# Attention: twelve copies of stacked queries and keys made by VectorE in place of ScalarE

## The chip, the cores and the metric

One core of a Trainium2 chip. The metric is the device time of one execution in microseconds. Of the kernel before there are three runs, and one execution more that the hardware profiler recorded.

## The reference, cut to what matters

A decoder layer: a mixer of four parallel groups (differential attention, a Conformer convolution, a short gated convolution, causal pooling) behind one input projection, an output projection, then an MLP with a squared ReLU. The change lies in the attention. It has 4 heads with two maps each; queries and keys have 32 elements a map, values 64 a head.

```python
sc = jnp.einsum('bhmqd,bhmkd->bhmqk', qi, k).astype(jnp.float32) * scale
mask = kpos[None, :] <= (st + jnp.arange(Q_BLOCK))[:, None]
p = jax.nn.softmax(jnp.where(mask, sc, -jnp.inf), axis=-1)
a = p[:, :, 0] - lam * p[:, :, 1]
return jnp.einsum('bhqk,bhkd->bhqd', a.astype(v.dtype), v)
```

The sequence has 2048 rows, so 16 row tiles of 128. Row tile i attends to i + 1 tiles of keys.

## The kernel before, in words

The kernel runs in phases: the input projection with the convolutions, attention, the output projection, the MLP. In attention a unit u is one head of one row tile (i = u // 4, head u % 4), and there are 64 of them. A loop over steps 0 to 66 is written out for each engine; each engine works its own list in order, and semaphores tie the lists together. In step u:

- **TensorE** (`score`, `turn`, `product`, and the loop below them) takes the score matmuls of unit u, one item for each map at first (L2421, with a mask product on the diagonal, L2424), and between them the items of `at_items(u)`: the transposes of `turn` (L2386). One kind of them, "stack", prepares the next row tile: in step u the quarter f = u % 4 of row tile u // 4 + 1, f = 0 and 1 its queries (four of the eight maps each), f = 2 and 3 its keys. The other kind, "at", transposes the attention weights of unit u - 3. Their PSUM banks, 4 and 5, alternate, so item n waits until item n - 2 has been read. `product` (L2401) multiplies the turned weights with the values, two items later.
- **VectorE** (`read_scores`, L1837) reads each score item out of PSUM, scales it and takes the row minimum; between the two reads it does `combine(u - 2)` (L1854, L1855, L1857), which makes a = p0 - ratio * p1. Behind the reads of steps 0 to 3 it runs taps of the convolution (`pump`, L1615, four in a step for u < 3, and the last one with two sums, L1626, in step 3), later parts of a layer norm (L1640, L1641, L1654, L1659).
- **ScalarE** takes the exponentials of unit u - 1 (`exp_of`, L1267) and between them the first half of the step's items (`read_turn`, L1258): each item is copied out of PSUM, a stack item into `q_stack` or `k_stack`, a weights item into `a_t`. The second half follows the second exponential. In some steps it also makes the rounded heads of the queries and keys (`split_head`, L1235), whose remainders POOL computes (L941), and in steps 7 and 8 the layer norm's square and root, with table loads.

Three waits hold this together. A score item waits until the item two before it has been read (`sc_read`). Before the first unit of a row tile TensorE waits until the tile's last stack item has been read. A turn waits for the read of the turn two before. All reads of turns raise one semaphore, `at_read`, whose count is the number of the item in `AT_ITEMS`.

The layer norm adds two items: column sums of 128x512 (L2298) at step 6 in place of a score, and at step 8 in place of a turn.

```python
for k in range(max(pairs, len(items))):
    if k < pairs:
        score(u, k)
    if k < len(items):
        turn(items[k])
        behind.append(items[k])
        if len(behind) > 2:
            product(behind.pop(0))
```

Of the kernel before, what the change touches and what calls it, by code (L numbers as in the profile page):

```python
# [23 lines left out]
P = 128  # L24
# [6 lines left out]
BLK = 512  # L31
# [68 lines left out]
UNITS = NT * HEADS  # L100
# [47 lines left out]
def running(counts):  # L148
    out = [0]
    for n in counts:  # L150
        out.append(out[-1] + n)
    return out
# [8 lines left out]
SC_NO = running(len(sc_items(u)) for u in range(UNITS))  # L161
AT_ITEMS = [x for u in range(-1, STEPS) for x in at_items(u)]
AT_POS = {x: n for n, x in enumerate(AT_ITEMS)}
PV_NO = running(len(at_groups(u)) for u in range(UNITS))
UPPER_NO = running(int(upper(u) < len(at_groups(u))) for u in range(UNITS))
SLOT = [3, 1, 2, 0]


def turned(u):
# [11 lines left out]
def trunk(nc, x, c, w_ada, b_ada, norm1_g, norm2_g, w_in, w_out, q_norm_g, k_norm_g, lam_params,  # L181
# [3 lines left out]
    with ctx:  # L185
# [7 lines left out]
        def sem(name):  # L193
# [149 lines left out]
        split_hi, split_lo = sem("split_hi"), sem("split_lo")  # L343
        sc_mm, sc_read, max_ready, exp_done, a_ready = [sem(n) for n in (
            "sc_mm", "sc_read", "max_ready", "exp_done", "a_ready")]
        at_mm, at_read, pv_mm, o_read = [sem(n) for n in ("at_mm", "at_read", "pv_mm", "o_read")]
        upper_ready = sem("upper_ready")
        asq_ready, ams_ready, arms_ready, arcp_ready, att_ready = [sem(n) for n in (
            "asq_ready", "ams_ready", "arms_ready", "arcp_ready", "att_ready")]
# [29 lines left out]

        def chan_no(h, cc, b):  # L380
            return (h * NB + b) * GC + cc

        def prob(u, m, c0, n):

# [46 lines left out]
        def ln_read(h, b, s):  # L431

            if (h, b) == (1, 1):
                return (at_read, AT_POS["ln", 1, 1] + 1) if s else (sc_read, SC_NO[LN_STEP] + 1)
            return (lnsd_ready if s else lnd_ready), h * NB + b + 1

        def released(o):
# [134 lines left out]
        def _(sp):  # L572
# [169 lines left out]

            def store_att(j):
                if j < LAST:
                    sp.wait_ge(at_read, AT_POS["att", j, 1] + 1)
                else:
                    sp.wait_ge(last_read, 2)
                src = att_t[j % 2] if j < LAST else att_t_last
                sp.dma_start(mix_v[:, 0:2, j * BLK:(j + 1) * BLK], src[:, :, :]).then_inc(attt_st[j % 2], 16)
# [242 lines left out]
        def _(act):  # L992
# [244 lines left out]
            def read_turn(x):  # L1237
                kind, i, f = x
                n = AT_POS[x]
                if kind == "ln":  # L1240
                    ln_root(1, 1)
                    return
                act.wait_ge(at_mm, n + 1)
                width = BLK
                if kind == "stack":
                    m0, width = 4 * (f % 2), BLK
                    src = at_bank(n).rearrange("p (m t) -> p m t", m=4)
                    dst = q_stack[i % 2][:, m0:m0 + 4, :] if f < 2 else k_stack[:, m0:m0 + 4, i * P:(i + 1) * P]
                elif kind == "att":
                    if i >= 2 and f == 0:  # L1250
                        act.wait_ge(attt_st[i % 2], 16)
                    src, dst = at_bank(n), att_t[i % 2][:, f, :]
                else:
                    gn, width = PV_NO[i] + f, at_groups(i)[f][1] * P
                    if gn >= 3:
                        act.wait_ge(pv_mm, gn - 2)
                    src, dst = at_bank(n)[:, 0:width], a_t[gn % 3][:, 0:width]
                A(dst, src, ACT.Copy).then_inc(at_read, 1)  # L1258
# [36 lines left out]
            for u in range(STEPS):  # L1295
                for n, a in splits_at(u):
                    split_head(n, a)
                if u == LN_STEP + 1:
                    ln_square(1, 1)
                if u in (LN_STEP + 10, LN_STEP + 11):  # L1300
                    ln_silu(1, 1, (u - LN_STEP - 10,))
                items = at_items(u)
                early = (len(items) + 1) // 2
                if 0 <= u - 1 < UNITS:
                    exp_of(u - 1, 0)
                for n, x in enumerate(items[:early]):
                    read_turn(x)
                    if u == UNITS + 1:
                        if n == 0:
                            act.wait_ge(sc_mm, SC_NO[UNITS])  # L1310
                        mix_head(n)
                if 0 <= u - 1 < UNITS:
                    exp_of(u - 1, 1)
                for n, x in enumerate(items[early:]):
                    if n == 0 and u == UNITS + 1:
                        wo_head(0, 0, (at_mm, turned(UNITS - 3)))
                    read_turn(x)
                if u == UNITS + 2:
                    wo_head(0, 1, (at_mm, turned(UNITS - 2)))
# [142 lines left out]
        def _(dve):  # L1462
# [397 lines left out]
            def read_o(i):  # L1860
                if i >= 8 and i % 4 == 0:
# [5 lines left out]
                                in1=inv_sum[:, i % 4, :].rearrange("p (a o) -> p a o", o=1).to_broadcast([P, HEADS, VD])  # L1867
                                ).then_inc(o_read, 1)

            def mix_tail(n):  # L1870
                tok = slice(n % HT * P, (n % HT + 1) * P)
                dve.wait_ge(mixhi_ready, n + 1)
                V.tensor_tensor(out=h_lo[:, :, tok], in0=mix_in[n % 2][:, :, :], in1=f32(h_hi[:, :, tok]),
                                op=ALU.subtract).then_inc(mix_ready, 1)
# [21 lines left out]
            for u in range(STEPS):  # L1896
                if u == FULL:
                    for b in range(NB):
                        dve.wait_ge(ln_st[b], 32)
                older = (lambda: combine(u - 2)) if 0 <= u - 2 < UNITS else (lambda: None)  # L1900
                if u < UNITS:
                    read_scores(u, older)
                else:
                    older()
                if u >= 8 and u % HEADS == 0 and u // HEADS - 2 < NT:
                    read_o(u // HEADS - 2)

                pump(taps, 4 if u < 3 else 9 * TAPS)
                if 0 <= u - LN_STEP - 3 < 4:
                    inverted = ln_inverse(u - LN_STEP - 3)  # L1910
                if 0 <= u - LN_STEP - 7 < GC:
                    ln_scale_part(u - LN_STEP - 7, inverted)
                j = att_stage(u, 1)
                if j is not None:
                    att_sums(j, att_sq)
                    first_guess(j)
# [286 lines left out]
        def _(pe):  # L2203
# [158 lines left out]
            def turn(x):  # L2362
                kind, i, f = x
                n = AT_POS[x]
                if n >= 2:
                    pe.wait_ge(at_read, n - 1)
                if kind == "ln":
                    ln_sum(1, 1, 1).then_inc(at_mm, 1)
                    return
                if kind == "stack":  # L2370
                    a = f // 2
                    pe.wait_ge(split_lo, 2 * i + a + 1)
                    src = f32((k_split if a else q_split)[:, :, :, :]).rearrange("p m s d -> p m (s d)")
                    srcs = [src[:, 4 * (f % 2) + m, :] for m in range(4)]
                elif kind == "att":
                    pe.wait_ge(att_ready, i + 1)
                    srcs = [att_tiles(i)[:, t, f * P:(f + 1) * P] for t in range(4)]
                else:
                    k0, nk = at_groups(i)[f]
                    if f == 0:  # L2380
                        pe.wait_ge(a_ready, i + 1)
                    if f == upper(i):
                        pe.wait_ge(upper_ready, UPPER_NO[i] + 1)
                    srcs = [prob(i, 0, (k0 + k) * P, P) for k in range(nk)]
                for m, src in enumerate(srcs):
                    ins = nc.tensor.transpose(at_bank(n)[:, m * P:(m + 1) * P], src, ident[:, :])  # L2386
                ins.then_inc(at_mm, 1)

            def product(x):
                kind, u, g = x  # L2390
                if kind != "at":
                    return
                i, hd = u // HEADS, u % HEADS
                gn, (k0, nk) = PV_NO[u] + g, at_groups(u)[g]
                pe.wait_ge(at_read, AT_POS[x] + 1)
                if u == 0:
                    pe.wait_ge(v_ld, 16)
                if hd == 0 and g == 0 and i >= 2:
                    pe.wait_ge(o_read, i - 1)
                for k in range(nk):  # L2400
                    ins = M(psum[:, 6 + i % 2, hd * VD:(hd + 1) * VD], a_t[gn % 3][:, k * P:(k + 1) * P],  # L2401
                            v_sb[:, k0 + k, hd * VD:(hd + 1) * VD], start=(k0 + k == 0), stop=(k0 + k == i),
                            skip_group_check=True)
                ins.then_inc(pv_mm, 1)
# [28 lines left out]
            for u in range(STEPS):  # L2433
                pairs, items = len(sc_items(u)), at_items(u)
                if u < UNITS and u % HEADS == 0:
                    pe.wait_ge(at_read, AT_POS["stack", u // HEADS, 3] + 1)
                for k in range(max(pairs, len(items))):
                    if k < pairs:
                        score(u, k)
# [19 lines left out]
                            skip_group_check=(t == 0))  # L2459
                return ins  # L2460

            pe.wait_ge(at_read, len(AT_ITEMS))
            for hc in range(2):
                n0 = hc * HT
                for t in range(HT):
# [148 lines left out]
```

## Time and profile before

| | us |
|---|---|
| median of three runs | 2356.99 |
| lowest, highest | 2356.3, 2362.84 |
| profiled execution | 2356.43 |
| its span | 2354.6 |
| attention, first score to last transposes | about 493 to 838 |
| granted TensorE clock, mean over the span | 0.993 |

Engines in the profile: PE is TensorE, PEld its weight loads, DVE VectorE, ACT ScalarE, POOL GpSimd, SPq the queue of DMAs that SyncE issues. A granted clock of 1.00 is 2.4 GHz, 0.50 is 1.2 GHz. In a timeline row the bracket gives the engine's idle time before the instruction and what ended it. A read with a minimum (TENSOR_SCALAR_CACHE_REDUCE) is followed by a short DVE_READ_ACCUMULATOR.

### The profile page before, as it was taken

How to read it: one execution, taken by the hardware profiler on the slowest of the kernel's cores; microseconds unless marked ns; L12 is line 12 of the kernel's file. 1: busy time of each engine (PE TensorE's matmuls, PEld its weight loads, DVE VectorE, ACT ScalarE, POOL GpSimd, SP SyncE). 2: the span in 40 equal slices, each digit the busy share in tenths (PEclk: the TensorE clock that was granted, in tenths of full speed). 3: DMA queues.
4: the chain of work that ended last, by engine and by line, in shares of the span. 5: the costliest groups of instructions: out<-in, count | busy, mean ns of one | idle time of the engine just before them, and what ended most of it. 6: DMA issues, size and time to landing. Idle time of an engine off the chain costs nothing.

```text
span 2354.6 us, 31383 instructions
## 1 busy us (share of the span) xinstructions
PE 2283.8 (97%) x11642; PEld 1924.3 (82%) x11642; DVE 1746.0 (74%) x2659; ACT 971.2 (41%) x1595; POOL 357.9 (15%) x285
## 2 busy tenths in 40 slices
PE   6999999988999999999999999999999999999999
PEld 5987898767889888888888888888888888888887
DVE  6648886889989876876767767676787676767676
ACT  4531555458888844332323232233432323222231
POOL 0442044824356610000000000000000000000000
PEclk9999999989999999999999999999999999999999
DMA  7441533120000152011111111145111111111112
GB/s 270 155 152 63 157 129 118 63 89 28 15 10 24 52 155 81 18 54 54 53 53 53 37 61 45 54 132 189 63 36 53 54 36 62 45 53 53 53 53 89
DMA packets 108280, 177.68 MB, mean 75 GB/s; under 512 B 5512, under 2 KB 77468, under 8 KB 107164
## 3 DMA queue, kind: packets, MB, share of 16 engines
q1 hardware_dynamic: 108100, 176.41, 22.6%
q8 instruction: 58, 0.95, 0.2%
q14 instruction: 34, 0.28, 0.0%
q10 hardware_dynamic: 88, 0.04, 0.0%
HBM read 152.84 MB, written 23.59 MB: 75 GB/s over the span
## 4 chain that ended last, share of the span: by engine, by line
PE 81%; DVE 10%; DMA 3%; issue 2%; ACT 2%; POOL 2%; SPq 0%; ACTq 0%; DVEq 0%; POOLq 0%
PE ps L2513 10%; PE ps L2512 10%; PE ps L2511 10%; PE ps L2550 8%; PE ps L2548 8%; PE ps L2549 8%; PE ps L2210 5%; PE ps L2212 5%; PE ps L2211 5%; PE ps L2401 3%; DVE ps L1615 2%; PE ps L2458 2%; PE ps L2456 2%; PE ps L2457 2%; DMA sb_w_raw<-in_w_in 2%
## 5 line engine op out<-in xcount | busy, mean ns | idle before, releaser
L1997 DVE TENSOR_TENSOR sb_x_new<-sb_x_new,ps 128x512 f32<-128x512 f32 x512 | 347.2, 684 | 107.5 <-PE ps L2513 102.0
L2511 PE MATMUL ps<-sb_w_hi,sb_u_hi 128*128 128x512 f32 x1024 | 398.3, 389 | 0.0
L2512 PE MATMUL ps<-sb_w_lo,sb_u_hi 128*128 128x512 f32 x1024 | 398.3, 389 | 0.0
L2513 PE MATMUL ps<-sb_w_hi,sb_u_lo 128*128 128x512 f32 x1024 | 398.3, 389 | 0.0
L2512 PEld LDWEIGHTS ps<-sb_w_lo,sb_u_hi 128*128 128x128 f32 x1024 | 192.2, 188 | 39.9
L2511 PEld LDWEIGHTS ps<-sb_w_hi,sb_u_hi 128*128 128x128 f32 x1024 | 192.2, 188 | 39.9
L2513 PEld LDWEIGHTS ps<-sb_w_hi,sb_u_lo 128*128 128x128 f32 x1024 | 192.2, 188 | 39.9
L2212 PE MATMUL ps<-sb_h_hi,sb_w_lo 128*128 128x512 f32 x512 | 199.4, 389 | 0.0
L1428 ACT ACTIVATE ps<-ps 128x512 f32<-128x512 f32 x28 | 16.3, 582 | 410.8 <-PE ps L2550 410.8
L2210 PE MATMUL ps<-sb_h_hi,sb_w_hi 128*128 128x512 f32 x448 | 177.5, 396 | 0.7 <-DVE sb_w_lo L1958 0.7
L2211 PE MATMUL ps<-sb_h_lo,sb_w_hi 128*128 128x512 f32 x448 | 174.4, 389 | 0.0
L2548 PE MATMUL ps<-sb_h_hi,sb_ring_hi 128*128 128x512 f32 x448 | 174.3, 389 | 0.0
L2549 PE MATMUL ps<-sb_h_lo,sb_ring_hi 128*128 128x512 f32 x448 | 174.3, 389 | 0.0
L1354 ACT ACTIVATE sb_u_hi<-sb_u_full 128x512 fp32r<-128x512 f32 x128 | 81.0, 632 | 192.0 <-DVE sb_u_full L1986 114.2
L1837 DVE TENSOR_SCALAR_CACHE_REDUCE sb_scores<-ps 128x1024 f32<-128x1024 f32 (+7 forms) x160 | 139.5, 891 | 12.4 <-PE ps L2424 6.9
L2401 PE MATMUL ps<-sb_v_sb,sb_a_t 128*128 128x64 f32 x1088 | 140.7, 270 | 0.0
L1615 DVE SCALAR_TENSOR_TENSOR ps<-sb_conf,sb_col,ps 128x512 f32<-128x512 f32 x208 | 140.4, 747 | 0.0
L2401 PEld LDWEIGHTS ps<-sb_v_sb,sb_a_t 128*128 128x128 f32 x1088 | 136.4, 195 | 0.5 <-ACT sb_q_stack L1258 0.2
L2421 PE MATMUL ps<-sb_k_stack,sb_q_stack 128*128 128x512 f32 (+3 forms) x320 | 112.8, 417 | 23.2 <-DVE sb_scores L1837 18.3
L2550 PE MATMUL ps<-sb_h_hi,sb_w_lo 128*128 128x512 f32 x336 | 130.7, 389 | 0.0
L2548 PE MATMUL ps<-sb_w_hi,sb_ring_hi 128*128 128x512 f32 x336 | 130.7, 389 | 0.0
L2549 PE MATMUL ps<-sb_w_lo,sb_ring_hi 128*128 128x512 f32 x336 | 130.7, 389 | 0.0
(291 smaller groups left out, 4947.9 us busy)
## 6 DMA issues: line engine op xcount, KB each, us to landing
sb_w_full<-in_w_ff SPq DMA_DIRECT2D x34, 1024.0 KB, 4.9
sb_w_full<-in_w_ff SPq DMA_DIRECT2D x56, 512.0 KB, 3.7
sb_w_raw<-in_w_in SPq DMA_DIRECT2D x16, 1024.0 KB, 5.6
sb_ada<-in_w_ada SPq DMA_DIRECT2D x32, 512.0 KB, 5.0
sb_ada_first<-in_w_ada SPq DMA_DIRECT2D x8, 1024.0 KB, 13.7
sb_x_in<-in_x SPq DMA_DIRECT2D x16, 512.0 KB, 5.4
sb_mix_in<-mix_scratch SPq DMA_DIRECT2D x16, 512.0 KB, 4.9
sb_x_new<-in_x SPq DMA_DIRECT2D x16, 512.0 KB, 4.9
```

Source lines behind the costliest of these rows:

```text
L1615: ins = V.scalar_tensor_tensor(out=dst, in0=src, scalar=w, in1=dst, op0=ALU.mult, op1=ALU.add)
L1997: V.tensor_tensor(out=y, in0=y, in1=psum[:, 4 + p % 4, :], op=ALU.add).then_inc(ff2_read, 1)
L2210: M(dst, ah, bh, start=(n == 0), stop=False)
L2211: M(dst, ah, bl, start=False, stop=False)
L2212: ins = M(dst, al, bh, start=False, stop=(n == last))
L2401: ins = M(psum[:, 6 + i % 2, hd * VD:(hd + 1) * VD], a_t[gn % 3][:, k * P:(k + 1) * P], v_sb[:, k0 + k, hd * VD:(hd + 1) * VD], start=(k0 ...
L2511: M(dst, uh, wh[:, j, col], start=j == order[0], stop=False, skip_group_check=fast)
L2512: M(dst, uh, wl[:, j, col], start=False, stop=False, skip_group_check=fast)
L2513: ins = M(dst, ul, wh[:, j, col], start=False, stop=j == order[1], skip_group_check=fast)
L2548: M(psum[:, bank, :], wh[:, k, :], rh[:, k, :], start=fresh and k == 0, stop=False, skip_group_check=True)
L2549: M(psum[:, bank, :], wh[:, k, :], rl[:, k, :], start=False, stop=False, skip_group_check=True)
L2550: ins = M(psum[:, bank, :], wl[:, k, :], rh[:, k, :], start=False, stop=k == DC // 2 - 1, skip_group_check=True)
```

## The change

A list `BY_DVE` marks twelve stack items: all four quarters of row tiles 1 and 2 and the key quarters (f = 2, 3) of row tiles 3 and 4. They fall in steps 0 to 7, 10, 11, 14 and 15. VectorE copies them (`copy_stack`) behind `combine(u - 2)`, between its score reads, and raises `stack_read`. ScalarE's list leaves them out, and is halved after leaving them out. Every wait for the read of a turn goes through `turn_read(n)`, which names the semaphore that counts item n and its number there. TensorE waits at the start of a row tile for both its last query quarter and its last key quarter.

```diff
+BY_DVE = [x[0] == "stack" and (1 <= x[1] <= 2 or 3 <= x[1] <= 4 and x[2] > 1) for x in AT_ITEMS]
+AT_BY_DVE = running(int(d) for d in BY_DVE)
...
+def stacks_of_dve(u):
+
+    return [x for x in at_items(u) if BY_DVE[AT_POS[x]]]
...
+        def stacked(i, f):
+
+            m0 = 4 * (f % 2)
+            return (at_bank(AT_POS["stack", i, f]).rearrange("p (m t) -> p m t", m=4),
+                    q_stack[i % 2][:, m0:m0 + 4, :] if f < 2 else k_stack[:, m0:m0 + 4, i * P:(i + 1) * P])
+
+        def turn_read(n):
+
+            by_dve = AT_BY_DVE[n + 1]
+            return (stack_read, by_dve) if BY_DVE[n] else (at_read, n + 1 - by_dve)
...
-                items = at_items(u)
+                items = [x for x in at_items(u) if not BY_DVE[AT_POS[x]]]
                 early = (len(items) + 1) // 2
...
+            def copy_stack(i, f):
+                src, dst = stacked(i, f)
+                dve.wait_ge(at_mm, AT_POS["stack", i, f] + 1)
+                V.tensor_copy(dst, src).then_inc(stack_read, 1)
...
-                older = (lambda: combine(u - 2)) if 0 <= u - 2 < UNITS else (lambda: None)
+                def older():
+                    if 0 <= u - 2 < UNITS:
+                        combine(u - 2)
+                    for x in stacks_of_dve(u):
+                        copy_stack(*x[1:])
+
                 if u < UNITS:
                     read_scores(u, older)
...
                 if n >= 2:
-                    pe.wait_ge(at_read, n - 1)
+                    pe.wait_ge(*turn_read(n - 2))
...
                 if u < UNITS and u % HEADS == 0:
-                    pe.wait_ge(at_read, AT_POS["stack", u // HEADS, 3] + 1)
+                    pe.wait_ge(*turn_read(AT_POS["stack", u // HEADS, 1]))
+                    pe.wait_ge(*turn_read(AT_POS["stack", u // HEADS, 3]))
```

The other waits for `at_read` (the layer norm's, `store_att`, `product`, and the one before the output projection) are rewritten with `turn_read` in the same way.

VectorE's list from the first score read on, steps 0 to 2, before (L1837 reads a score, L1615 is a convolution tap):

```order
L1837 TENSOR_SCALAR sb_scores_128,sb_part_min<-ps 128x128 [waits sc_mm,proj_ready]
L1837 TENSOR_SCALAR sb_scores_128,sb_part_min<-ps 128x128 [waits sc_mm]
L1615 SCALAR_TENSOR_TENSOR ps<-sb_conf,sb_col_55,ps 128x512 [waits dve_chain] x4
L1837 TENSOR_SCALAR sb_scores_128,sb_part_min<-ps 128x128 [waits sc_mm] x2
L1615 SCALAR_TENSOR_TENSOR ps<-sb_conf,sb_col_55,ps 128x512 [waits dve_chain] x4
L1837 TENSOR_SCALAR sb_scores_129,sb_part_min<-ps 128x128 [waits sc_mm]
L1854 RECIPROCAL sb_ratio<-sb_exp_sum 128x1 [waits exp_done]
L1855 SCALAR_TENSOR_TENSOR sb_ratio<-sb_exp_sum,sb_ratio,sb_small 128x1 [waits dve_chain]
L1857 SCALAR_TENSOR_TENSOR sb_scores_128<-sb_scores_128,sb_ratio 128x128 [waits dve_chain]
```

and now, from the first copy on (L1853 reads a score, L1889 is the copy):

```order
L1889 CAST sb_q_stack_136<-ps 128x512 [waits at_mm]
L1853 TENSOR_SCALAR sb_scores_128,sb_part_min<-ps 128x128 [waits sc_mm]
L1631 SCALAR_TENSOR_TENSOR ps<-sb_conf,sb_col_55,ps 128x512 [waits dve_chain] x4
L1853 TENSOR_SCALAR sb_scores_128,sb_part_min<-ps 128x128 [waits sc_mm]
L1889 CAST sb_q_stack_136<-ps 128x512 [waits at_mm]
L1853 TENSOR_SCALAR sb_scores_128,sb_part_min<-ps 128x128 [waits sc_mm]
L1631 SCALAR_TENSOR_TENSOR ps<-sb_conf,sb_col_55,ps 128x512 [waits dve_chain] x4
L1853 TENSOR_SCALAR sb_scores_129,sb_part_min<-ps 128x128 [waits sc_mm]
L1870 RECIPROCAL sb_ratio<-sb_exp_sum 128x1 [waits exp_done]
L1871 SCALAR_TENSOR_TENSOR sb_ratio<-sb_exp_sum,sb_ratio,sb_small 128x1 [waits dve_chain]
L1873 SCALAR_TENSOR_TENSOR sb_scores_128<-sb_scores_128,sb_ratio 128x128 [waits dve_chain]
L1889 CAST sb_k_stack<-ps 128x4x128 [waits at_mm]
```

A copy stands between the two reads of each step, behind the combination where there is one.

TensorE's list from the last key quarter of row tile 1 (step 3) to the second score of step 4, before (L2386 transposes, L2421 is a score, L2424 its mask product):

```order
L2386 MATMUL ps<-sb_ident,sb_k_split 128x128 [waits split_lo,at_read]
L2386 MATMUL ps<-sb_ident,sb_k_split 128x128 x3
L2421 MATMUL ps<-sb_k_stack,sb_q_stack_135 128x128 [waits sc_read]
L2424 MATMUL ps<-sb_mask_r,sb_ident_r 128x128
L2386 MATMUL ps<-sb_ident,sb_scores_128 128x128 [waits a_ready,at_read]
L2421 MATMUL ps<-sb_k_stack,sb_q_stack_136 128x256 [waits sc_read,at_read]
L2424 MATMUL ps<-sb_mask_r,sb_ident_r 128x128
L2386 MATMUL ps<-sb_ident,sb_q_split 128x128 [waits split_lo,at_read]
L2386 MATMUL ps<-sb_ident,sb_q_split 128x128 x3
L2421 MATMUL ps<-sb_k_stack,sb_q_stack_136 128x256 [waits sc_read]
L2424 MATMUL ps<-sb_mask_r,sb_ident_r 128x128
```

and now:

```order
L2412 MATMUL ps<-sb_ident,sb_k_split 128x128 [waits split_lo,stack_read]
L2412 MATMUL ps<-sb_ident,sb_k_split 128x128 x3
L2447 MATMUL ps<-sb_k_stack,sb_q_stack_135 128x128 [waits sc_read]
L2450 MATMUL ps<-sb_mask_r,sb_ident_r 128x128
L2412 MATMUL ps<-sb_ident,sb_scores_128 128x128 [waits a_ready,stack_read]
L2447 MATMUL ps<-sb_k_stack,sb_q_stack_136 128x256 [waits sc_read,stack_read]
L2450 MATMUL ps<-sb_mask_r,sb_ident_r 128x128
L2412 MATMUL ps<-sb_ident,sb_q_split 128x128 [waits split_lo,stack_read]
L2412 MATMUL ps<-sb_ident,sb_q_split 128x128 x3
L2447 MATMUL ps<-sb_k_stack,sb_q_stack_136 128x256 [waits sc_read]
L2450 MATMUL ps<-sb_mask_r,sb_ident_r 128x128
```

Nothing has moved; the first score of row tile 1 (128x256) and the transposes around it now wait for `stack_read`, which VectorE raises.

## Rows read from the trace of the kernel before

**Rows 1.** the page, busy time: us, share of the span, instructions
```profile
PE 2283.8 (97%) x11642; PEld 1924.3 (82%) x11642; DVE 1746.0 (74%) x2659; ACT 971.2 (41%) x1595; POOL 357.9 (15%) x285
```

**Rows 2.** stretches: length, busy PE, PEld, DVE, ACT, POOL, clock, DMA share, GB/s
```profile
485.00:506.20 21.20, 14.38 (x73) 11.86 (x71) 20.92 (x46) 11.99 (x29) 9.30 (x8) 0.74 0.60 196
506.20:512.90 6.70, 6.68 (x23) 4.81 (x24) 2.76 (x14) 4.27 (x15) 1.27 (x1) 0.54 0.17 48
...
523.20:541.30 18.10, 13.36 (x92) 10.89 (x92) 17.64 (x48) 14.76 (x40) 3.82 (x3) 1.00 0.06 16
```

**Rows 3.** chain of waits, 486 to 560 us: start us, us, what
```profile
495.25 2.64 DVE ps L1615 x4
...
498.30 2.64 DVE ps L1615 x4
...
506.22 0.58 PE ps L2421
...
512.91 0.69 DVE sb_acc L1640
...
515.77 0.60 ACT sb_scores L1267 x2
...
523.18 0.17 DVE sb_ratio L1854
...
541.34 0.03 ACT sb_scores L1267
```

**Rows 4.** TensorE alone, microsecond stretches: busy time, granted clock, DMA share
```profile
492.00:493.00 1.00, 0.00 (x0) 1.00 0.00 0
...
495.00:496.00 1.00, 0.91 (x5) 0.63 0.83 313
...
512.00:513.00 1.00, 1.00 (x7) 0.84 0.00 0
```

**Rows 5.** ScalarE's copy line; then timeline of VectorE: start us, us, instruction
```profile
L1258 ACT ACTIVATE sb_k_stack<-ps x32: 573/580/610, 490.7 to 781.6; 128x512 fp32r<-128x512 f32 x32
...
483.49 0.48 DVE L1697 TENSOR_SCALAR sb_stage<-sb_prod,sb_col 128x512 f32<-128x512 f32 x1
...
509.12 0.42 DVE L1837 TENSOR_SCALAR_CACHE_REDUCE sb_scores<-ps 128x256 f32<-128x256 f32 x1
...
536.99 0.68 DVE L1837 TENSOR_SCALAR_CACHE_REDUCE sb_scores<-ps 128x512 f32<-128x512 f32 x1
537.60 0.08 DVE L1837 DVE_READ_ACCUMULATOR sb_scores<-ps 128x1 f32 x1
```

**Rows 6.** timeline of TensorE and VectorE, steps 3 to 5
```profile
504.28 0.55 PE L2421 MATMUL ps<-sb_k_stack,sb_q_stack 128*128 128x256 f32 x1 [0.96 <-DVE sb_scores L1837]
...
504.50 1.46 DVE L1857 SCALAR_TENSOR_TENSOR sb_scores<-sb_scores,sb_ratio 128x128 f32<-128x128 f32 x1
...
504.73 1.08 PE L2386 MATMUL ps<-sb_ident,sb_q_split 128*128 128x128 f32 x4
...
508.81 0.35 DVE L1857 SCALAR_TENSOR_TENSOR sb_scores<-sb_scores,sb_ratio 128x128 f32<-128x128 f32 x1
```

**Rows 7.** timeline of VectorE, step 6, with its idle time before
```profile
512.91 0.69 DVE L1640 TENSOR_TENSOR sb_acc<-sb_acc,ps 128x512 f32<-128x512 f32 x1 [3.36 <-PE ps L2298]
```

**Rows 8.** timeline of ScalarE, steps 6 and 7
```profile
516.38 0.60 ACT L1258 ACTIVATE sb_k_stack<-ps 128x512 fp32r<-128x512 f32 x1
...
518.15 0.50 ACT L1267 ACTIVATE sb_scores<-sb_scores,sb_part_min 128x256 f32<-128x256 f32 x1
```

**Rows 9.** timeline of VectorE (two rows) and ScalarE, steps 9 to 15
```profile
525.99 1.26 DVE L1855 SCALAR_TENSOR_TENSOR sb_ratio<-sb_exp_sum,sb_ratio,sb_small 128x1 f32<-128x1 f32 x1
...
537.60 1.36 DVE L1659 TENSOR_TENSOR sb_acc<-sb_acc,sb_ln_rs 128x512 f32<-128x512 f32 x1
...
542.06 0.57 ACT L1258 ACTIVATE sb_k_stack<-ps 128x512 fp32r<-128x512 f32 x1
```

More of the change, by code:

```diff
@@ L345, in trunk @@
             "sc_mm", "sc_read", "max_ready", "exp_done", "a_ready")]
-        at_mm, at_read, pv_mm, o_read = [sem(n) for n in ("at_mm", "at_read", "pv_mm", "o_read")]
+        at_mm, at_read, stack_read, pv_mm, o_read = [sem(n) for n in ("at_mm", "at_read", "stack_read", "pv_mm", "o_read")]
         upper_ready = sem("upper_ready")
@@ L433, in ln_read @@
             if (h, b) == (1, 1):
-                return (at_read, AT_POS["ln", 1, 1] + 1) if s else (sc_read, SC_NO[LN_STEP] + 1)
+                return turn_read(AT_POS["ln", 1, 1]) if s else (sc_read, SC_NO[LN_STEP] + 1)
             return (lnsd_ready if s else lnd_ready), h * NB + b + 1
@@ L744, in store_att @@
                 if j < LAST:
-                    sp.wait_ge(at_read, AT_POS["att", j, 1] + 1)
+                    sp.wait_ge(*turn_read(AT_POS["att", j, 1]))
                 else:
@@ L1245, in read_turn @@
                 if kind == "stack":
-                    m0, width = 4 * (f % 2), BLK
-                    src = at_bank(n).rearrange("p (m t) -> p m t", m=4)
-                    dst = q_stack[i % 2][:, m0:m0 + 4, :] if f < 2 else k_stack[:, m0:m0 + 4, i * P:(i + 1) * P]
+                    src, dst = stacked(i, f)
                 elif kind == "att":
@@ L1868, in read_o @@
                                 ).then_inc(o_read, 1)
+            def copy_stack(i, f):
+                src, dst = stacked(i, f)
+                dve.wait_ge(at_mm, AT_POS["stack", i, f] + 1)
+                V.tensor_copy(dst, src).then_inc(stack_read, 1)
             def mix_tail(n):
@@ L2394, in product @@
                 gn, (k0, nk) = PV_NO[u] + g, at_groups(u)[g]
-                pe.wait_ge(at_read, AT_POS[x] + 1)
+                pe.wait_ge(*turn_read(AT_POS[x]))
                 if u == 0:
@@ L2460, in out_part @@
                 return ins
-            pe.wait_ge(at_read, len(AT_ITEMS))
+            pe.wait_ge(*turn_read(len(AT_ITEMS) - 1))
             for hc in range(2):
```

## The prediction

> **What bounds the kernel now.** I read the busy shares first: TensorE works 97% of the span and VectorE 74% [rows 1]. Those are averages over very different stages, and the change touches only steps 0 to 15 of attention, about 493 to 552 us. So the next view is the stretches of just that part [rows 2]. There VectorE is the busy one: 20.92 of 21.20 us up to 506.2 and 17.64 of 18.10 us from 523.2 to 541.3. TensorE has gaps in both. The chain of waits says who ends last [rows 3]. It stays on VectorE through the convolution taps and the score reads until 506.2, passes to TensorE (scores, transposes, then the four column sums of L2298) until 512.9, to VectorE until 515.8, to ScalarE until 523.2, to VectorE until 541.3, and then to ScalarE. The third view is TensorE's granted clock [rows 4]. It fell from 2.4 to 1.2 GHz in the microsecond 495 to 496, after TensorE had done nothing from 492 to 493, and it was 0.84 on average in 512 to 513, so it came back at about 512.3, after TensorE had worked without a gap since 506.2.
>
> The change moves twelve of ScalarE's 64 stack copies (32 of them into k_stack [rows 5]), 0.58 us each, to VectorE. For most of them the engine that gives the work away is not on the chain, and the engine that takes it is. I therefore expect a small loss.
>
> **The price of one copy.** No copy from PSUM runs on VectorE before. The nearest row is L1837 on 128x512 from PSUM: 0.68 us long, but the next instruction starts 0.61 us after it [rows 5]. On 256 columns it takes 0.42 us [rows 5], so the slope is 1.0 ns a column and reading PSUM is not done at a double rate. I take 0.62 us of VectorE's time a copy, with 0.61 and 0.69 as ends. A floor from afar is 0.48 us, L1697 on 128x512 from SBUF, which I keep for the range alone.
>
> The Trainium skill (VectorE: DVE Perf Modes, the section on the TRN2 errata) gives 120 cycles plus one a column for VectorE out of PSUM and 172 plus one for ScalarE with its faster clock; as an estimate from that page a copy would cost 0.66 us on VectorE against 0.57 on ScalarE, a rule that speaks against the change and would raise the sum by 0.3 us. The trace has 0.58 for ScalarE and shows no such copy on VectorE.
>
> **The sum, step by step.** The copy of step u stands between the two score reads of that step, behind the combination of u-2.
> - Steps 0, 1, 2: VectorE has no idle time and is on the chain [rows 3], so 3 x 0.62 = 1.86 us, all paid.
> - Step 3: the copy of the last keys of row tile 1 starts when L1857 ends, at 505.96 (504.50 plus 1.46), and ends at 506.58. Scores of step 4 need it. Before, TensorE did the first score of step 4, its mask product and the four transposes from 504.28 to 505.81, in VectorE's shadow [rows 6]. Now these 1.53 us come after the copy: the second score starts at 506.62 + 1.53 = 508.15 instead of 506.22, a loss of 1.93 us. TensorE is at half clock there. If the clock comes back after the same unbroken work as before, the extra 1.53 us are in effect done at full clock at the end of the stretch, which returns 0.76. Net 1.17.
> - Steps 4, 5: nothing. Two copies, 1.24 us, lie beside TensorE's column sums; VectorE idles 3.36 us before L1640 [rows 7]. Without that cover they would cost 1.24.
> - Step 6: the copy stands before both reads, because the extra item makes three of them; VectorE is on the chain from 512.91 to 515.8. 0.62.
> - Step 7: VectorE's read of the second score ends 0.62 later, which uses up the half microsecond that it had until ScalarE's exponential at 518.15 [rows 8]. The scores of step 8 wait for this copy instead of ScalarE's, which had ended at 516.98 [rows 8]. About 0.3, since ScalarE with its two table loads is the chain here.
> - Steps 10, 11, 14: VectorE is on the chain; 3 x 0.62 = 1.86. ScalarE's three copies had stood beside its own waits, so nothing is given back.
> - Step 15: off VectorE's part of the chain, which had passed to ScalarE at 541.34. ScalarE loses a copy of 0.58, but its list is now cut in the middle after leaving the stacks out, so a_t comes before the second exponential and waits for transposes of its own step. Of the 0.58 I count 0.15 as gained.
>
> 1.86 + 1.17 + 0 + 0.62 + 0.3 + 1.86 - 0.15 = 5.66, so 5.7 us. Nothing behind step 16 can give it back: no load is late there and the order is fixed. DMAs, SP's and POOL's queues keep their content. The extra wait that TensorE issues before each row tile, for the queries' copy, is satisfied long before the keys' one. The profiled execution took 2356.43 us (span 2354.6), so 2362.1 us; the median of the three runs is 0.56 us above it.
>
> **Clock, weighed again.** In the rows the clock came back after unbroken work. The Trainium skill (TensorE: Matmul & The Clock Gate, Part 1) has the activity watched by a free-running measure, so that the moment need not follow the start of the work. If it returned at the same 512.3 us as before, while the work starts at 508.5 (506.62 plus the 1.86 of steps 0 to 2), then of 8.7 us of work counted at half clock (1.53, the 6.1 before the clock came back, and 0.55 after it, which is 1.1) 3.8 would be done at half clock and the rest in 2.45. It would end at 514.75 where it ended at 512.85, so steps 0 to 5 would lose 1.9 instead of 3.0, and the sum would be 4.5.
>
> **The rivals.**
> *Slower by over 0.3% (chance 0.30): the late hand-over.* Each row tile's first scores now wait for a copy that stands late in VectorE's list. I charge this only at step 4. If there is no slack behind it elsewhere either, step 8 costs 0.56 more (its score 1.5 us later than ScalarE's copy allowed, of which 0.62 is counted in step 6 and 0.3 in step 7), step 12 costs 0.35 and step 16 1.05 (VectorE's copy would end at 544.17, ScalarE's ended at 542.63 [rows 9]; 0.5 of the difference lies under work that waits anyway), and a clock that doesn't return within the sums costs 1.3 more. Together 3.3, so 9.0 us and 2365.4. It passes the bound once 1.4 of the 3.3 is real. For it speaks that TensorE waits for VectorE at nearly every score; against it that VectorE's own next read comes later still at steps 12 and 16.
> *No slower (chance 0.15): the holds go.* A VectorE instruction with two SBUF inputs stands still while POOL's L941 runs: L1857 took 1.46 us at 504.50 against 0.35 at 508.81 [rows 6]. The same happens at 525.99 (L1855, 1.26 where it otherwise takes about 0.2) and at 537.60 (L1659, 1.36 against 0.69) [rows 9]. POOL's start follows ScalarE, and VectorE is now 0.6 us and more later against it. If all three miss POOL, 1.11 + 1.04 + 0.67 = 2.8 us return, and with the early clock (1.1) the loss is 1.8: 2358.2. It turns to a gain only if ScalarE's two copies on the chain, at 516.38 and 542.06, return their 0.5 us each and one more microsecond is found. New holds are as likely as lost ones, hence the low chance.
> *The forecast (chance 0.55)*: 2359.5 to 2364.
>
> That the change doesn't do what it says is excluded by the two orders: twelve copies are on VectorE's list and gone from ScalarE's.
>
> **The numbers.** 0.3% is 7.1 us, about what a measurement of this kernel can tell from no change. Slower by more holds 0.85 of the first rival and some 0.08 of the forecast: 0.30. Faster by more needs 7.1 us from copies that total 7.0 on ScalarE: 0.04, for what I don't see. Within: 0.66. The range reaches into both rivals, 2357.5 to 2366.5.
>
> **What would show it.** Right: twelve copies near 0.62 to 0.68 us on VectorE; the chain on VectorE in steps 0 to 3 with each step 0.6 us longer (period 3.06 to 3.7); the first score of step 4 later than 506.22 + 1.86; VectorE's copies of steps 4 and 5 inside its wait for L2298; the start of the projection after attention 4 to 7 us later and the time after it unchanged. Wrong: copies under 0.5 us; the clock at 2.4 GHz earlier than 512; long holds that have come or gone; or a chain that in 523 to 541 has left VectorE.

## The result and the profile after

The median of 20 runs is 2363.49 us, against 2358.22 us for 20 runs of the kernel before on the same chips. Three of these forty runs came in a slower state (3005.7, 3224.17 and 3815.12 us), and the ratio leaves them out: 1.0028, with a 95% interval of 1.0018 to 1.0037. So the change makes the kernel slower, by 6.6 us (4.2 to 8.7); the two medians alone lie 5.3 us apart. The prediction was 2362.1 us, 5.7 us more than its profiled execution. The profiled execution of the changed kernel took 2363.48 us. Run to run, both kernels scatter by several microseconds, and the profiles of the experiments show part of the reason.

The page's first part answers to [rows 1]: twelve instructions have moved and VectorE is 6.1 us busier.

```profile
PE 2286.7 (97%) x11642; PEld 1926.7 (82%) x11642; DVE 1752.1 (74%) x2671; ACT 965.6 (41%) x1583; POOL 358.5 (15%) x285
```

VectorE's copy line of the changed kernel, with who waited for it (us in total, times):

```profile
L1889 DVE CAST sb_k_stack<-ps x8: 677/682/684, 505.7 to 553.3; 128x512 fp32r<-128x512 f32 x8
L1889 DVE CAST sb_q_stack<-ps x4: 683/684/686, 497.6 to 515.0; 128x512 fp32r<-128x512 f32 x4
...
  PE ps L2447: 6.2, 3
...
  PE ps L2412: 3.3, 2
```

A copy lasts 0.68 us, as L1837 did in [rows 5]. TensorE waited for it for 6.2 us before three scores and for 3.3 us before two groups of transposes. The timeline of VectorE in step 0 gives the price on VectorE: the next read starts 0.60 us after the start of the copy.

```profile
497.44 0.28 DVE L1853 TENSOR_SCALAR_CACHE_REDUCE sb_scores<-ps 128x128 f32<-128x128 f32 x1
...
497.65 0.69 DVE L1889 CAST sb_q_stack<-ps 128x512 fp32r<-128x512 f32 x1
498.25 0.28 DVE L1853 TENSOR_SCALAR_CACHE_REDUCE sb_scores<-ps 128x128 f32<-128x128 f32 x1
```

That first read had begun at 494.74 before, so the profiled execution was 2.70 us late before any changed instruction ran. To keep such things apart I use one measure from here on: the start of the first score read of each unit in VectorE's timeline, less its start in the first profile of the kernel before, less the same difference for unit 0. It shows what has been lost inside attention since the first read.

| unit | 1 | 2 | 3 | 4 | 5 | 6 | 7 | 8 | 9 | 10 | 12 | 14 | 15 | 16 | 20 to 28 |
|---|---|---|---|---|---|---|---|---|---|---|---|---|---|---|---|
| changed kernel | 0.6 | 1.2 | 1.8 | 2.8 | 3.2 | 2.2 | 2.2 | 3.4 | 5.8 | 5.2 | 6.4 | 6.0 | 7.0 | 8.0 | 6.9 to 7.1 |

So 6.9 us are lost in the steps that the change touches, and the growth is very uneven. Part of the unevenness goes with the granted clock. TensorE of the changed kernel in stretches of 2 us (length, busy time, granted clock, DMA share, GB/s), answering to [rows 4]:

```profile
512.00:514.00 2.00, 2.00 (x12) 0.50 0.07 25
514.00:516.00 2.00, 2.00 (x11) 0.76 0.03 8
...
520.00:522.00 2.00, 1.48 (x12) 0.95 0.00 0
522.00:524.00 2.00, 1.13 (x5) 0.50 0.00 0
524.00:526.00 2.00, 2.00 (x7) 0.50 0.26 45
...
538.00:540.00 2.00, 0.31 (x3) 0.71 0.00 0
540.00:542.00 2.00, 2.00 (x9) 0.50 0.08 26
```

The stretch at 1.2 GHz that began at about 498 ends at 515.0 (0.76 on average in 514 to 516), and then the clock falls twice more, near 522 and near 538. Before, it stayed at 2.4 GHz from 512.3 to 829.8. TensorE's timeline shows the long wait of step 4, the two scores beside the later falls, each waiting for a copy, and what the clock does to the column sums of step 8:

```profile
510.93 0.55 PE L2447 MATMUL ps<-sb_k_stack,sb_q_stack 128*128 128x256 f32 x1 [3.40 <-DVE sb_k_stack L1889]
...
522.87 0.66 PE L2447 MATMUL ps<-sb_k_stack,sb_q_stack 128*128 128x384 f32 x1 [1.07 <-DVE sb_k_stack L1889]
...
524.72 3.72 PE L2324 MATMUL ps<-sb_ln_sq,sb_ones_mean 128*128 128x512 f32 x4
...
539.87 0.77 PE L2447 MATMUL ps<-sb_k_stack,sb_q_stack 128*128 128x512 f32 x1 [1.69 <-DVE sb_k_stack L1889]
```

The group of four column sums took 1.93 us before and takes 3.72 now. ScalarE needs their result, so its timeline has a wait there that the kernel before didn't have (its L1087 started at 520.55 without idle time):

```profile
528.48 0.69 ACT L1105 ACTIVATE sb_ln_rs<-ps,sb_small 128x512 f32<-128x512 f32 x1 [2.05 <-PE ps L2324]
```

### The profile page after: what moved, and what is told of

Same layout as the page of the kernel before. It is cut to its first block, busy times and chain, and to the rows that moved or that the text cites. A ratio compares the mean times of both kernels' runs of the same rounds, so it can differ in the third digit from the quotient of the medians.

```text
span 2361.7 us, 31385 instructions
## 1 busy us (share of the span) xinstructions
PE 2286.7 (97%) x11642; PEld 1926.7 (82%) x11642; DVE 1752.1 (74%) x2671; ACT 965.6 (41%) x1583; POOL 358.5 (15%) x285
## 4 chain that ended last, share of the span: by engine, by line
PE 81%; DVE 10%; DMA 3%; issue 2%; POOL 2%; ACT 2%; SPq 0%; DVEq 0%; ACTq 0%; POOLq 0%
PE ps L2539 10%; PE ps L2538 10%; PE ps L2540 10%; PE ps L2577 8%; PE ps L2576 8%; PE ps L2575 8%; PE ps L2236 5%; PE ps L2238 5%; PE ps L2237 5%; PE ps L2427 2%; DVE ps L1631 2%; PE ps L2485 2%; PE ps L2483 2%; PE ps L2484 2%; PE ps L2412 2%
## 5 line engine op out<-in xcount | busy, mean ns | idle before, releaser
L1853 DVE TENSOR_SCALAR_CACHE_REDUCE sb_scores<-ps 128x1024 f32<-128x1024 f32 (+7 forms) x160 | 139.9, 892 | 16.9 <-PE ps L2450 10.5
```

## The experiments

Three theories were set against each other. A is the prediction's: VectorE's own time on the chain, and the late hand-over at step 4. B: a starved TensorE falls to 1.2 GHz and that makes up a good part of the loss. C: ScalarE's list, cut at another place, costs time. The numbers called shift are the measure above, each from one profile, and "the end" means units 20 to 28, behind the last copy that is moved.

**The kernel before, twice more.** The same kernel without an edit, for what belongs to chance.

> The kernel before again, for a second profile. If the clock's falls outside steps 0 to 16 (near 463, 772 and 830 to 856 us) are chance and no work of the change, they come or stay away here too: the first read of scores may lie up to 3 us later than at 494.74, while the distances between the reads of units 0 to 20 stay within 1 us of the first profile's.

> The kernel before a third time, for the same question as the second: which falls of TensorE's clock belong to the kernel and which to chance. Units 0 to 20 within 1 us of the first profile's distances.

Their executions took 2362.7 and 2359.57 us. The first reads came 2.69 and 2.96 us later than in the first profile, as in the changed kernel. The cause is a fall of the clock near 463, in a row like this of the second profile (TensorE, stretches of 2 us and, lower down, of 4 us):

```profile
464.00:466.00 2.00, 2.00 (x4) 0.58 0.35 131
...
772.00:776.00 4.00, 4.00 (x19) 0.50 0.01 4
836.00:840.00 4.00, 4.00 (x24) 0.55 0.92 295
```

Over all fourteen profiles the first read is 2.2 to 3.0 us late where the clock fell near 463 and 0.1 to 0.4 us late where it didn't. The shifts are 0.0 up to unit 5 in both. From unit 6 to unit 50 they are -1.4 in the second profile, where the clock was back at 2.4 GHz earlier beside the column sums of step 6, and +0.1 to +0.2 in the third. I had expected them within 1 us; the -1.4 is a miss, and it says how much one return of the clock is worth. The falls near 463, 772 and 836 come with the kernel before too, so they don't need the change. Between steps 6 and 16 none of its three profiles has a fall. The late falls show in the time: from the first read to the start of the output projection the three profiles of the same program took 345.68, 349.96 and 345.87 us.

**The changed kernel again.**

> The changed kernel again. Theory A: the shifts of units 0 to 16 repeat within 0.5 us. Theory B: they repeat up to unit 7, and from there on differ by 1 us or more if the granted clock falls at other places than 522 and 538 us; what lies before the first score (2.70 us later in the first profile) and at the end of attention (2.8 us given back) is chance and comes out otherwise.

Shifts 0.6, 1.2, 1.8, 2.8, 3.2, then 2.1 at unit 6, 3.4 at unit 8, 5.7 at unit 9, 5.2 at unit 10, 8.0 at unit 16 and 6.9 at the end; the clock fell near 521 and 538. They repeat within 0.1 to 0.2 us, and the kernel with ScalarE's order kept (below) has the same two falls. None of the three profiles of the kernel before has them, so they belong to the change. What I had called chance outside attention repeated as well, against my expectation: the first read came 2.20 us late, and 2.8 us were given back behind the end. The ratio was 1.0044 (1.0029 to 1.0059), medians 2371.15 against 2358.97 us. Its nine runs lie in two groups, 2360.8 to 2364.0 and 2371.2 to 2375.6 us; the profiled one was among the faster. What the other group pays more I haven't seen in a trace.

**Row tile 1 alone.**

```diff
-BY_DVE = [x[0] == "stack" and (1 <= x[1] <= 2 or 3 <= x[1] <= 4 and x[2] > 1) for x in AT_ITEMS]
+BY_DVE = [x[0] == "stack" and (x[1] == 1) for x in AT_ITEMS]
```

> VectorE copies only row tile 1's four quarters (steps 0 to 3). Theory A (VectorE's own time on the chain, and the late hand-over at step 4): first reads of units 1, 2, 3 later by 0.6, 1.2, 1.8 us, and from unit 6 on a constant shift near the 2.2 us that the changed kernel shows at unit 6, at most the 3.0 of the prediction; so 2.2 to 3.0 us slower in all. Theory B (the loss comes from TensorE's clock, which falls to 1.2 GHz more often when TensorE is starved): the same start, but with stretches at half clock between 517 and 548 us and a shift of 4 or more by unit 16. Theory C (ScalarE's changed order): the shift already over 0.6 a step in steps 1 to 3.

Shifts 0.6, 1.2, 1.8, 2.8 and 3.2 for units 1 to 5, as in the changed kernel, then 1.5 from unit 6 to unit 23. The first four copies and the hand-over at step 4 cost 3.2 us, and half of that is given back beside the column sums of step 6. That is below the 2.2 I had set as the lower end; the 2.2 of the changed kernel holds the copy of step 6 besides, and is 1.6 without it. The clock was down from 528.7 to 532.1 without any cost to the shift. The ratio is 1.0020 (1.0011 to 1.0029).

**Row tile 2 alone** (the same line with `x[1] == 2`).

> VectorE copies only row tile 2's four quarters (steps 4 to 7). Theory A: steps 4 and 5 cost nothing (shift at unit 6 is 0.0), steps 6 and 7 together 0.9 us. Theory B: up to 3 us, if the clock falls while the scores of step 8 wait for the copy, so that the column sums of step 8 take 3.5 us instead of 1.9. A shift over 0.5 at unit 6 would speak against the cover that the prediction named.

Shift 0.9 at unit 6, 1.2 at unit 7, 2.4 at unit 8, 3.9 at unit 9, 3.4 from unit 10 on. The 0.9 at unit 6 passes the 0.5 that I had set as a sign against the cover. The sign was badly chosen: the copy of step 6 stands ahead of that read and takes 0.6 of it, and units 4 and 5 came at 0.0 and 0.1, so the cover of steps 4 and 5 held. Theory A's 0.9 for the whole is refuted. Most of the rest goes with the clock, which fell at 516.3, but not as theory B had it: TensorE stood idle for 1.34 us before the first score of step 7, and before the first score of step 8, which did wait for the copy, only for 0.16. That score and the column sums of step 8:

```profile
519.28 0.66 PE L2447 MATMUL ps<-sb_k_stack,sb_q_stack 128*128 128x384 f32 x1 [0.16 <-DVE sb_k_stack L1889]
...
521.13 2.91 PE L2324 MATMUL ps<-sb_ln_sq,sb_ones_mean 128*128 128x512 f32 x4
```

The ratio is 1.0030 (1.0019 to 1.0041).

**The key quarters of row tiles 3 and 4 alone** (`3 <= x[1] <= 4 and x[2] > 1`).

> VectorE copies only the key quarters of row tiles 3 and 4 (steps 10, 11, 14, 15). Theory A: 0.6 us each in steps 10, 11, 14, nothing in 15, so a shift of 1.7 us from unit 16 on. Theory B: the same plus what a fall of the clock in 530 to 546 costs, 1 us or more. No loss (below 0.5) would speak against both.

This execution had the early return of the clock, -1.0 at units 6 to 10. From there it went to -0.4, 0.2, 0.5 and 1.1 at units 11, 12, 14 and 15: 2.1 us, near the 1.7 of theory A. The clock was down from 530.8 to 534.2 meanwhile. Then it was down again from 541.0 to 554.7, the shift rose to 5.6 and stayed at 4.9, so theory B has it here. This fall begins where transposes start to wait for a copy:

```profile
542.14 1.11 PE L2412 MATMUL ps<-sb_ident,sb_k_split 128*128 128x128 f32 x4 [1.16 <-DVE sb_k_stack L1889]
```

So these four copies cost 5.9 us inside attention in this execution. The ratio is 1.0013 (1.0004 to 1.0021), 3 us.

**All but the last key quarter.**

```diff
+BY_DVE = [x[0] == "stack" and (x[2] < 3 and (1 <= x[1] <= 2 or 3 <= x[1] <= 4 and x[2] > 1)) for x in AT_ITEMS]
```

> As the changed kernel, but ScalarE keeps the last key quarter (f = 3) of every row tile, the one that the next tile's first score waits for; eight copies stay on VectorE. Theory A: step 3 loses its copy and its late hand-over (1.17 to 1.9 us), step 7 its 0.3, step 11 its 0.62: 3.7 us slower than before in all, against 5.7 predicted and 6.9 seen inside attention. Theory B: the falls of the clock near 522 and 538 are gone with the two waits for the copy (1.07 and 1.69 us), and the shift by unit 16 is below 4. Were the hand-over free, the shift by unit 16 would be 5 or more.

Shift 1.8, 1.7, 1.8 at units 3 to 5, 1.6 at units 6 to 10, 3.4 at unit 16, 2.9 at the end. The step from 1.8 to 2.8 at unit 4 is gone with the late hand-over. The clock still fell, near 528 and 545, but late enough to cost nothing in step 8. The end is 4.0 us better inside attention than the changed kernel for four copies fewer, which at 0.6 us explain 2.4 at most; with the late hand-over theory A had counted 3.7 for the end, theory B below 4 by unit 16, so this run doesn't part the two. In time it doesn't show: 1.0033 (1.0021 to 1.0045), with six runs, and falls near 772 and 836 in the profile.

**ScalarE's order kept.**

```diff
-                early = (len(items) + 1) // 2
+                early = sum(not BY_DVE[AT_POS[x]] for x in at_items(u)[:(len(at_items(u)) + 1) // 2])
```

> As the changed kernel, but ScalarE's list is cut in the middle as before the change, so that a_t stays behind the second exponential. Theory A and B: within 0.7 us of the changed kernel. Theory C (ScalarE's new order costs): 1 us or more faster than the changed kernel, the shift by unit 16 below 6.

Shifts 2.3, 3.6, 6.1 at units 6, 8, 9, 8.2 at unit 16 and 7.0 at the end; 1.0033 (1.0021 to 1.0045). The same as the changed kernel. Theory C falls.

**Every copy twice.**

```diff
-                V.tensor_copy(dst, src).then_inc(stack_read, 1)
+                link(V.tensor_copy(dst, src))
+                V.tensor_copy(dst, src).then_inc(stack_read, 1)
```

> As the changed kernel, but VectorE makes each of its twelve copies twice, one behind the other, and releases after the second. Theory A: each further copy costs its 0.61 to 0.68 us where the first did, in eight steps (0, 1, 2, 3, 6, 10, 11, 14), so 5 to 5.5 us more than the changed kernel, 11 to 13 us slower than before; period of steps 0 to 2 3.65 becomes 4.3 us. If VectorE's time is covered and only the hand-over counts: 2 us more or less.

Up to unit 3 the shift is 4.0 instead of 1.8, so 0.7 us a step for the second copy, as theory A has it. Then 8.4 at unit 6, 13.2 at unit 9, 20.6 at the end, with TensorE at half clock until 520, from 523 to 534, 544 to 551 and 558 to 571. The total is 1.0087 (1.0073 to 1.0102), 20.5 us, where eight paid copies explain 11 to 13. This speaks against theory A alone. How much of the rest is the clock and how much the later hand-over, which the second copy delays in every row tile, this run doesn't tell.

**The copy in front of the combination.**

```diff
+                    for x in stacks_of_dve(u):
+                        copy_stack(*x[1:])
                     if 0 <= u - 2 < UNITS:
                         combine(u - 2)
-                    for x in stacks_of_dve(u):
-                        copy_stack(*x[1:])
```

> As the changed kernel, but the copy of step u stands in front of the combination of u - 2. VectorE's work is the same, the hand-over 0.9 us earlier, and more in step 3, where a hold of the combination by POOL no longer lies ahead of the copy. Theory A: TensorE's 1.5 us of step 4 begin before the hold ends; 1.0 to 1.8 us faster than the changed kernel, some 4 us slower than before. Theory B: also the wait of 1.07 us before step 8 shrinks and the clock stays up near 522. If the hand-over is free: the same as the changed kernel within 0.5.

The same twelve copies, and the shift is 1.8, 1.8, 1.9 at units 3 to 5, 1.7 at units 6 and 7, 2.2 at units 8 and 9, 3.6 at unit 16 and 2.9 at the end, 4.0 us less than the changed kernel. More than theory A's 1.0 to 1.8. The wait before step 8 has shrunk to 0.24 us, and the clock stayed up:

```profile
521.34 0.42 PE L2447 MATMUL ps<-sb_k_stack,sb_q_stack 128*128 128x384 f32 x1 [0.24 <-DVE sb_k_stack L1889]
...
522.81 1.93 PE L2324 MATMUL ps<-sb_ln_sq,sb_ones_mean 128*128 128x512 f32 x4
```

The ratio is 1.0028 (1.0018 to 1.0038), the same as the change's. In the same series the changed kernel had 1.0044 (1.0029 to 1.0059); the intervals overlap, so a gain in time isn't shown. The profile has falls near 463, 772 and 836.

**TensorE kept busy while it waits.** The wait for the stack moves behind the score's own wait, and between the two stand eight matmuls whose results the score overwrites.

```diff
                 if r >= 2:
                     pe.wait_ge(sc_read, r - 1)
+                if u in (8, 12) and k == 0:
+                    for _ in range(8):
+                        M(psum[:, 2 * (r % 2), 0:2 * P], ident_r[:, :], k_stack[:, 0, 0:2 * P], start=True, stop=True,
+                          skip_group_check=True)
+                if u < UNITS and u % HEADS == 0 and k == 0:
+                    pe.wait_ge(*turn_read(AT_POS["stack", u // HEADS, 1]))
+                    pe.wait_ge(*turn_read(AT_POS["stack", u // HEADS, 3]))
```

> As the changed kernel, but TensorE does eight more matmuls of 256 columns, whose results are overwritten, where it would wait for VectorE's copy in steps 8 and 12. Theory B (an idle TensorE loses its clock near 522 and 538, which costs 3.6 us between units 7 and 9): although TensorE has more work, the clock stays at 2.4 GHz there, the column sums of step 8 take 1.9 us instead of 3.5, and the shift from unit 9 on is at least 2 us below the changed kernel's 5.8. Theory A (only VectorE's time and the late hand-over count): the shift at unit 9 is 5.8 or, with the added work in the way, up to 0.5 more.

The clock stayed up in step 8, and that gives the price of its fall. The timeline and the clock of the filled kernel:

```profile
521.84 1.19 PE L2440 MATMUL ps<-sb_k_stack,sb_ident_r 128*128 128x256 f32 x8
523.16 0.41 PE L2454 MATMUL ps<-sb_k_stack,sb_q_stack 128*128 128x384 f32 x1
...
524.14 1.93 PE L2324 MATMUL ps<-sb_ln_sq,sb_ones_mean 128*128 128x512 f32 x4
```

```profile
522.00:524.00 2.00, 1.88 (x16) 1.00 0.00 0
524.00:526.00 2.00, 2.00 (x9) 1.00 0.14 31
```

The same copies, more work on TensorE, and the shift goes 2.6, 3.6, 3.5, 3.1 at units 6, 8, 9, 10, where the changed kernel has 2.2, 3.4, 5.8, 5.2. So the clock's fall costs 2.3 us there. This is theory B's price.

That the filling is what kept the clock up isn't shown. In the changed kernel the fall comes at 521.8 (0.89 on average in 521 to 522), and TensorE's last work before the wait of 1.07 us, which the filling replaces, ends at 521.80:

```profile
520.32 0.39 PE L2447 MATMUL ps<-sb_k_stack,sb_q_stack 128*128 128x256 f32 x1 [1.34 <-DVE sb_scores L1853]
...
521.47 0.33 PE L2427 MATMUL ps<-sb_v_sb,sb_a_t 128*128 128x64 f32 x2
...
521.00:522.00 1.00, 0.80 (x8) 0.89 0.00 0
```

The second profile of the changed kernel has the fall at 521.2 and the start of the wait at 521.26; only with ScalarE's order kept does the wait begin 0.3 us ahead of the fall. What lies ahead of all these falls, and of the one of row tile 2 alone, is the idle time of 1.34 us before the first score of step 7. In the kernel before it is 0.74:

```profile
515.44 0.39 PE L2421 MATMUL ps<-sb_k_stack,sb_q_stack 128*128 128x256 f32 x1 [0.74 <-DVE sb_scores L1837]
```

That score waits for a read which now stands behind the copy of step 6, and the copy's 0.60 us is the difference:

```profile
519.24 0.68 DVE L1889 CAST sb_k_stack<-ps 128x512 fp32r<-128x512 f32 x1
```

The kernels without a fall there, filled, copy first and all but the last key quarter, have the same 1.34 us and next to no wait before step 8. So the wait before step 8 may still have a part in it, but one profile of each doesn't decide, and the cause of this fall stays open. Near 538 the wait of 1.69 us does begin ahead of the fall, by 0.6 to 1.0 us in the three profiles.

At step 12 the filling didn't hold the clock up throughout: it was down from 536.1 to 539.5. A later fall from 553 to 560, which nothing was put against, took the shift from 4.9 at unit 15 to 7.6 at the end, and the ratio is 1.0038 (1.0024 to 1.0052).

**VectorE copies only where the chain was elsewhere** (steps 5, 8, 16 and 17; ScalarE's order kept).

```diff
+BY_DVE = [x[0] == "stack" and (4 * (x[1] - 1) + x[2] in (5, 8, 16, 17)) for x in AT_ITEMS]
```

> VectorE makes only the stack copies of steps 5, 8, 16 and 17, where the chain of waits of the kernel before ran on TensorE or ScalarE; ScalarE's list is cut as before. Theory A: step 5 free, steps 8, 16 and 17 take 0.5 us each off ScalarE's part of the chain, so 0.5 to 1.5 us faster than before. If ScalarE's part can't be shortened by its copies, because VectorE is next in line at once, the same as before within 0.5 us inside attention.

Shift -1.4 at the end, the value that the kernel before had in its second profile. Here too the clock was back early, and -1.0 us of it stood at units 6 to 8 already, as in the kernel with the key quarters of row tiles 3 and 4. From there on 0.4 us are gained, less than theory A's 0.5 at least, and within the 0.5 us of the other reading. The ratio is 1.0008 (0.9999 to 1.0018). No gain in time is shown; no version tried beats the kernel before.

## Why the prediction held, and where its working was off

**Bound and sign: right.** VectorE was on the chain in steps 0 to 3 [rows 2, 3], ScalarE wasn't, and each copy of steps 0, 1 and 2 was paid in full: 0.6, 1.2, 1.8 against 3 x 0.62 = 1.86. The price was right too, 0.60 from the start of a copy to the next instruction, 0.68 long, as L1837 from PSUM and not as the 0.48 of L1697 from SBUF [rows 5]. The page's estimate of 0.66 us against 0.57 (the Trainium skill, VectorE: DVE Perf Modes, TRN2 errata) fits the 0.68 and 0.58 that the rows show as durations; what VectorE's list pays is the 0.60.

**Step 3, hand-over to step 4: the mechanism right.** It was the longest wait for a copy, 3.40 us before the score at 510.93. POOL's hold of [rows 6] stayed (L1873 took 1.24 us ahead of that copy). Keeping ScalarE's last quarter, or placing the copy before the combination, removed the step from 1.8 to 2.8 at unit 4.

**Clock in the column sums of step 6: the size off.** The prediction had 3.0 us lost by the sums' end. The changed kernel's L1656 starts at 517.19, 1.58 us later than before once the 2.70 of unit 0 are taken off; with step 6's copy that is the 2.2 at unit 6.

```profile
517.19 0.69 DVE L1656 TENSOR_TENSOR sb_acc<-sb_acc,ps 128x512 f32<-128x512 f32 x1 [1.20 <-PE ps L2324]
```

The clock came back at 515.0, 4.0 us after TensorE had begun to work without a gap at 510.93; before, it had taken 6.1 us, from 506.22 to 512.3. The assumption of the same unbroken work was wrong. Less the 2.70 of unit 0, 515.0 is 512.3 again. The other reading, by the Trainium skill (TensorE: Matmul & The Clock Gate, Part 1), that the moment doesn't follow the start of the work, fits better: it took the same 512.3 and gave 1.9. The kernel before in its second profile agrees: unbroken work from 508.90, the clock back at 512.1, 3.2 us later, and a shift of -1.4 from the moment alone.

**Steps 4 and 5: free, as said.** Row tile 2 alone shows 0.0 and 0.1 at units 4 and 5. VectorE's idle time before the sums' reader went from 3.36 [rows 7] to 1.20 us.

**Step 7: the term that failed.** It stood at 0.3 us, and units 7 to 10 went from 2.2 to 5.2. The copy of step 6 widened an idle time of TensorE from 0.74 to 1.34 us, the clock fell at 521.8, and the late copy of step 7 left TensorE idle for another 1.07 us. Everything in step 8 ran at 1.2 GHz, the sums took 3.72 us, and ScalarE waited 2.05 us for them. The filled kernel shows 2.3 us of this to be the clock. Where the clock stayed up, units 7 to 10 grew by 0.5 us (filled) and 0.1 us (copy first), so the 0.3 for the step without a fall was about right. The prediction asked whether the clock would come back, and never whether it would fall again.

**Steps 10, 11, 14, 15: right in sum.** 1.86 - 0.15 = 1.7 was predicted; units 10 to 20 and on go from 5.2 to 6.9. That the sum fits is partly luck too. The clock fell near 538, which no term had, and a hold went: L1659 had taken 1.36 us at 537.60 [rows 9], and its counterpart missed POOL and took 0.69:

```profile
546.95 0.69 DVE L1675 TENSOR_TENSOR sb_acc<-sb_acc,sb_ln_rs 128x512 f32<-128x512 f32 x1
```

This is the step from 6.6 at unit 13 to 6.0 at unit 14, in both profiles of the changed kernel and with ScalarE's order kept. With the clock up and the hold in place, in the kernel with the copy first, the same stretch took 1.1 us. In the kernel with these four copies alone the fall at 541.0 took the shift 3.8 us further from unit 15 to the end.

**The total.** 1.6 + 0.6 + 3.0 + 1.7 = 6.9 us inside attention in place of 5.7. That it lies close is partly luck: 1.4 too much in the sums of step 6, 2.7 too little in step 7. And the parts do not add up: row tile 1 alone, row tile 2 alone and the four key quarters alone cost 4.7, 7.1 and 3.1 us by their ratios, 14.9 together, where the whole costs 6.6. The whole is not firm either: measured again it cost 10.4 us (6.8 to 13.9). What I can show is that falls of the clock far behind the change, near 772 and 836, come or stay away from profile to profile, and the kernel before has them too. From first read to projection, less the shift inside attention and less the first profile's 345.68, the profiles show: the kernel before 0, +5.7, 0.0; the change -2.6 and -2.8; tile 1 +6.4, tile 2 +6.5, keys -2.8, copy first +2.0, where ScalarE is on the chain +5.2. The 2.6 to 2.8 us less are the profiles without any fall between 760 and 860; the first profile of the kernel before has one from 829.8 to 836.6. So the changed kernel's projection starts 7.0 us later than in the first profile: 2.7 us from ahead of the first read, 6.9 from the changed stretch, and 2.6 back behind it. The time after that start is 1514.2 us in both, as predicted. Whether a shift of a few microseconds makes such a late fall likelier, or it is chance, stays open: one profile for each kernel doesn't tell.

**The rivals.** The late hand-over as I had priced it (9.0 us) put 0.56 us more on step 8, where the clock's fall took 2.3; what it put on steps 12 and 16 can't be told from the fall near 538. Of the three holds of the other rival two stayed (L1873 at 508.99, L1871 at 533.92 with 1.25 us), and the one of L1659 went, with the 0.67 us that the rival gave it. One more that the prediction didn't name went too: L1855 had taken 1.25 us at 518.37 before, in step 8.

## What to carry to other kernels

Work given to the engine that the chain runs on costs its start-to-start time, once for each place where it has no cover, and the rows before tell that to a tenth of a microsecond. What they don't tell at a glance is the second effect: a copy that another engine waits for belongs as early in the list as its input allows. A late one idled TensorE here for 3.40, 1.07 and 1.69 us, and the clock fell beside the last two. Moving the copy ahead of the combination left 2.9 of the 6.9 us inside attention, though no gain in time was shown. For changes under 0.3%, compare positions inside the changed stretch between profiles of both kernels, and profile the old kernel more than once before an offset elsewhere is called an effect.

## What had not been expected of the hardware

In the changed kernel the clock fell at 521.8 although TensorE had stood idle for no longer than 0.53 and 1.34 us in the microseconds before, and with row tile 2 alone it fell inside the 1.34 us. With the same two gaps it stayed up there in three other kernels, one profile each. The return after a fall took 3.2 us of unbroken work in one profile of the kernel before, 6.1 us in another, and 4.0 us in the changed kernel. One program's time between two fixed points of its list varied from 345.7 to 350.0 us with the places at which the clock fell.
